# Expert weights in 2 MB transfers, in another order, with h2 stored as the gather reads it

## The reference

```python
logits = (x @ w_router + b_router)
top_vals, top_idx = lax.top_k(logits, TOP_K)            # 4 of 32 experts
wts = jax.nn.softmax(top_vals, axis=-1)
combine = jnp.sum(one_hot(top_idx, 32) * wts[..., None], axis=1)
def expert(acc, xs):
    wu, bu, wd, bd, g = xs                              # wu 1024 x 2048, wd 1024 x 1024
    gu = x @ wu + bu
    gate, up = gu[:, :D_FF], gu[:, D_FF:]
    gate = jnp.minimum(gate, 7.0)
    up = jnp.clip(up, -7.0, 7.0)
    glu = gate * jax.nn.sigmoid(1.702 * gate)
    y = ((up + 1.0) * glu) @ wd + bd
    return acc + g[:, None] * y, None
```

## Time and profile before

| | us |
|---|---|
| median of three runs | 1164.95 (1164.49 to 1165.76) |
| the profiled execution, its own time | 1163.09 |
| its span, first to last instruction | 1161.3 |
| TensorE busy in the span | 1112.6 |
| VectorE, ScalarE, GpSimd busy | 330.3, 168.0, 63.2 |
| mean rate of the DMA engines | 395 GB/s |

### The profile page before, as it was taken

How to read it: one execution, slowest core, us unless ns; L and a number is a source line. 1 busy time by engine, 2 the same in 40 slices (tenths; PEclk the granted TensorE clock), 3 DMA queues, 4 the chain that set the end, 5 groups by cost and what they waited for, 6 DMA issues and landing times.

```text
span 1161.3 us, 14218 instructions
## 1 busy us (share of the span) xinstructions
PE 1112.6 (96%) x5882; PEld 564.9 (49%) x5882; DVE 330.3 (28%) x622; ACT 168.0 (14%) x303; POOL 63.2 (5%) x107
## 2 busy tenths in 40 slices
PE   7999999989999999999999999999999999999996
PEld 6977799844444444444444444444444444444432
DVE  4675886422121212121212121212121212121113
ACT  4453145210000000000000000000000000000001
POOL 5040000100000000000000000000000000000000
PEclk9999999999999999999999999999999999999999
DMA  9989987878999999999999999999999999999992
GB/s 309 377 236 349 389 292 319 342 303 343 390 432 431 430 431 432 432 433 433 431 432 432 431 431 429 430 432 433 433 433 431 433 430 432 431 430 428 432 420 99
DMA packets 42609, 459.28 MB, mean 395 GB/s; under 512 B 3508, under 2 KB 15864, under 8 KB 26728
## 3 DMA queue, kind: packets, MB, share of 16 engines
q1 hardware_dynamic: 40936, 455.12, 94.0%
q0 software_dynamic: 1168, 2.81, 0.9%
q10 hardware_dynamic: 464, 0.79, 0.2%
HBM read 457.12 MB, written 1.57 MB: 395 GB/s over the span
## 4 chain that ended last, share of the span: by engine, by line
PE 47%; DMA 46%; DVE 2%; SPq 2%; issue 1%; ACT 1%; POOL 1%; POOLq 0%; DVEq 0%; ACTq 0%
DMA arena<-in_w_down_dram 41%; PE ps L1744 19%; PE ps L1705 12%; PE ps L1685 3%; DMA ring<-in_w_in_dram 3%; PE ps L1733 2%; DMA ring<-in_w_ada_dram 1%; DMA ring<-in_rpb_dram 1%; PE ps L1439 1%; SPq L401 1%; PE ps L1440 1%; PE ps L1607 1%; PE ps L1441 1%; SPq L397 1%; PE ps L1631 1%
## 5 line engine op out<-in xcount | busy, mean ns | idle before, releaser
L1705 PE MATMUL ps<-ring,arena 128*64 128x512 f32 x2048 | 452.4, 594 | 0.8 <-ACT arena L824 0.8
L1705 PEld LDWEIGHTS ps<-ring,arena 128*64 128x64 f32 x2048 | 143.5, 137 | 267.7 <-issue 261.2
L1744 PE MATMUL ps<-arena,x 128*64 128x512 f32 x992 | 219.2, 594 | 21.1 <-DMA arena<-in_w_down_dram 21.0
L1744 PEld LDWEIGHTS ps<-arena,x 128*64 128x64 f32 x992 | 70.6, 137 | 168.2 <-issue 133.4
L1685 PE MATMUL ps<-arena 128*128 128x128 f32 x512 | 124.9, 398 | 0.0
L1685 PEld LDWEIGHTS ps<-arena 128*128 128x128 f32 x512 | 121.9, 328 | 1.2 <-issue 1.2
L1243 DVE TENSOR_SCALAR arena<-iota,cur 128x128 f32<-128x128 f32 x64 | 19.3, 344 | 286.2 <-PE ps L1715 283.0
L1250 DVE TENSOR_SCALAR x<-ps 128x512 f32<-128x512 f32 x32 | 22.1, 692 | 257.0 <-PE ps L1705 257.0
L1265 DVE TENSOR_TENSOR late<-ps,gtf 128x512 f32<-128x512 f32 x64 | 41.2, 686 | 145.3 <-PE ps L1744 145.3
L615 POOL COPY selbuf<-sel 96x64 bf16 (+1 forms) x32 | 21.3, 665 | 871.4 <-DVE x L1251 868.9
L1733 PE MATMUL ps<-late,arena 64*128 64x512 f32 x264 | 65.9, 617 | 1.5 <-DVE late L1265 1.5
(11 more groups left out here) (267 smaller groups left out, 861.0 us busy)
## 6 DMA issues: line engine op xcount, KB each, us to landing
ring<-in_w_up_dram SPq DMA_DIRECT2D x58, 4096.0 KB, 27.1
arena<-in_w_down_dram SPq DMA_DIRECT2D x29, 4096.0 KB, 21.8
ring<-in_w_up_dram SPq DMA_DIRECT2D x12, 2048.0 KB, 12.4
ring<-in_w_ada_dram SPq DMA_DIRECT2D x16, 1024.0 KB, 10.8
ring<-in_w_ada_dram SPq DMA_DIRECT2D x16, 512.0 KB, 10.1
ring<-in_w_in_dram SPq DMA_DIRECT2D x16, 512.0 KB, 9.7
ring<-in_w_in_dram SPq DMA_DIRECT2D x8, 1024.0 KB, 7.5
arena<-in_w_down_dram SPq DMA_DIRECT2D x3, 2048.0 KB, 13.3
```

Source lines behind the costliest of these rows:

```text
L1705: ins = mm(ps[CAP * h:CAP * h + CAP, half, :].rearrange("q (p j) -> q p j", j=4), xgT[:, place, kk, CAP * a:CAP * a + CAP], w[:, half, :, ...
L1744: ins = mm(ps[CAP * n:CAP * n + CAP, YB, :], hT[:, j, CAP * h:CAP * h + CAP], w[:, jj, n * HALF:(n + 1) * HALF], start=(jj == 0), stop=(jj ...
```

## The change

Four edits go together.

1. All expert transfers up to D(30)'s first half are halves, 2 MB with runs of 16 KB. A half is issued when its own half of the place is free, and has its own semaphore: TensorE waits for the second half of U at kk = 2 and 6 and for the second half of D between the halves of `down`.
2. The order is U(e,0), U(e,1) for rising e, with D(e) after chunk u = 2e + `ahead(e)`, where u counts the chunks of w_up: after U(e+2,1) for e below 4, after U(e+2,0) for 4 to 9, and after U(e+1,1) from 10 on, which is the order in which TensorE reads them.
3. `h2` is stored with the columns dealt by j, so that the gather's weights are 128 adjacent floats; ScalarE's copy and `h2_out` write with a step instead.
4. After `up(0)` TensorE goes on to `up(1)`. `turn_hidden(0)`, the gather that stood after expert 0 (now into the bank of `down`'s result, YB) and, in the first round, the first scatter stand between the block rows of `up(1)`. The fixed parts of the loops change with it: 8 experts ahead of the loop and 4 behind it.

```diff
-HALVED = {(0, 0): 0, (0, 1): 0, (1, 0): 0, (1, 1): 0, (2, 0): 1, (E_LAST, 1): 1}
-FIRST_BODY = 4
+FIRST_BODY, LAST_BODY = 8, 4
+EVEN_FROM, EVEN_TO = 10, E - 4
+UP_HALVES = [(e, c) for e in range(E_LAST + 1) for c in range(2)]
+DOWN_HALVES = list(range(E_LAST))
+def ahead(e):
+    return 5 if e < 4 else 4 if e < EVEN_FROM else 3
+def order(first, last):
+    chunks = []
+    for u in range(2 * first, 2 * last):
+        chunks.append(("up", u // 2, u % 2))
+        chunks += [("down", e, None) for e in range(1, E) if 2 * e + ahead(e) == u]
+    return chunks
...
-                def up_whole(e, parity, c, after):
-                    sp.wait_ge(moe_free, after)
-                    sp.dma_start(up_chunk(parity, c).rearrange("p a b -> p (a b)"),
-                                 w_up_v[e, :, c, :]).then_inc(up_loaded[2 * parity + c][0], 16)
-                def down_whole(e, after):
-                    sp.wait_ge(moe_free, after)
-                    sp.dma_start(down_buf.rearrange("p a b -> p (a b)"), w_down_v[e, :, :]).then_inc(down_loaded[0], 16)
+                def up_whole(e, parity, c, at):
+                    for h in range(2):
+                        sp.wait_ge(moe_free, at + (2 * c + h + 1))
+                        sp.dma_start(up_chunk(parity, c)[:, 2 * h:2 * h + 2, :].rearrange("p a b -> p (a b)"),
+                                     w_up_v[e, :, c, 2 * h * SLOT:2 * (h + 1) * SLOT])\
+                            .then_inc(up_loaded[2 * parity + c][h], 16)
+                def down_whole(e, at):
+                    for h in range(2):
+                        sp.wait_ge(moe_free, at + (5 + h))
+                        down_part(e, 4 * h, 4 * h + 4, down_loaded[h])
+                def fixed(chunks):
+                    for kind, e, c in chunks:
...
+                fixed(order(2, EVEN_FROM + 2))
                 with sp.Fori(0, LOAD_LOOPS) as i:
...
                     for h in range(LOAD_BODY):
-                        steady(e0 + h, h, at0 + 6 * h)
+                        for c in range(2):
+                            up_whole(e0 + (h + 2), h, c, at0 + 6 * h)
+                        down_whole(e0 + (h + 1), at0 + 6 * (h + 1))
+                fixed(order(EVEN_TO + 2, E)[:-1])
...
-                        ins = nc.scalar.activation(h2[:, t, :].rearrange("p (a b) -> p a b", a=2),
-                                                   ps[:, 2 + 2 * t:4 + 2 * t, :], ACT.Copy)
+                        ins = nc.scalar.activation(h2[:, t, :].rearrange("p (a j q) -> p a q j", a=2, j=4),
+                                                   ps[:, 2 + 2 * t:4 + 2 * t, :].rearrange("p a (q j) -> p a q j", j=4),
+                                                   ACT.Copy)
...
-                V.scalar_tensor_tensor(out=h2[:, t, c], in0=ps[:, AF_BANK[k], :], scalar=rstd[:, t:t + 1],
-                                       in1=h2[:, t, c], op0=ALU.mult, op1=ALU.add).then_inc(h2_ready, 1)
+                by_row = h2[:, t, c].rearrange("p (j q) -> p q j", j=4)
+                V.scalar_tensor_tensor(out=by_row, in0=ps[:, AF_BANK[k], :].rearrange("p (q j) -> p q j", j=4),
+                                       scalar=rstd[:, t:t + 1], in1=by_row, op0=ALU.mult,
+                                       op1=ALU.add).then_inc(h2_ready, 1)
...
-                        ins = mm(ps[:, bank, j * P:(j + 1) * P], h2[:, t, HALF * c + j:HALF * (c + 1):4],
+                        ins = mm(ps[:, bank, j * P:(j + 1) * P], h2[:, t, HALF * c + j * P:HALF * c + (j + 1) * P],
...
-                    if kk % 4 == 2 and (e, c) in HALVED:
-                        per = 2 if c == e % 2 else 1
-                        pe.wait_ge(up_loaded[2 * (e % 2) + c][1], 16 * (r * per + HALVED[e, c] + 1))
+                    if kk % 4 == 2:
+                        pe.wait_ge(up_loaded[2 * (e % 2) + c][1], laps)
...
+                    elif e == 1:
+                        if kk == 2:
+                            turn_hidden(g - 1)
+                        if kk == 4:
+                            gather(r * PAIRS + 2, 0, YB)
+                        if kk == 5 and r == 0:
+                            scatter(g - 2, scat_done)
+                        if kk == 6:
+                            turn_weights(g - 1)
...
             def step(e, g, n, laps, loads, r):
                 up(e, g, laps, r, r == 0 and e == 0)
-                if e:
-                    down(e - 1, g - 1, loads)
+                if not e:
+                    return
+                if e == 1:
+                    pe.wait_ge(xg_ready, g + 2)
+                down(e - 1, g - 1, loads)
```

More of the change, by code:

```diff
@@ new lines, in down_whole @@
+                def down_whole(e, at):
[4 more added lines that the diff above has]
+                    for kind, e, c in chunks:
+                        if kind == "up" and (e, c) in UP_HALVES:
+                            for h in range(2):
+                                sp.wait_ge(moe_free, R + freed(e - 2) + 2 * c + h + 1)
+                                up_part(e, c, h)
+                        elif kind == "up":
+                            up_whole(e, e % 2, c, R + freed(e - 2))
+                        elif e in DOWN_HALVES:
+                            for h in range(2):
+                                sp.wait_ge(moe_free, R + freed(e) + 5 + h)
+                                down_part(e, 4 * h, 4 * h + 4, down_loaded[h])
+                        else:
+                            down_whole(e, R + freed(e))
@@ L447, in stream @@
                 first_free = [(O_done, 1), (kv_stored, 32), (unit_ready, 24), (unit_ready, 24), (br_done, KB),
                               (unit_ready, 28), (unit_ready, 32), (out_done, KB)]
-                order = [(0, 0, 0), (0, 0, 1), (0, 1, 0), (0, 1, 1), (1, 1, 1), (1, 0, 1), (1, 0, 0), (1, 1, 0)]
-                for (s, count), part in zip(first_free, order):
+                parts_of = [(0, 0, 0), (0, 0, 1), (0, 1, 0), (0, 1, 1), (1, 1, 1), (1, 0, 1), (1, 0, 0), (1, 1, 0)]
+                for (s, count), part in zip(first_free, parts_of):
@@ L457, in stream @@
                     down_part(0, 4 * h, 4 * h + 4, down_loaded[h])
[L458 to L470, removed]
+                fixed(order(2, EVEN_FROM + 2))
                 with sp.Fori(0, LOAD_LOOPS) as i:
-                    e0 = sp.snap(i * LOAD_BODY + 2)
-                    at0 = sp.snap(i * (6 * LOAD_BODY) + (R + freed(2)))
+                    e0 = sp.snap(i * LOAD_BODY + EVEN_FROM)
+                    at0 = sp.snap(i * (6 * LOAD_BODY) + (R + freed(EVEN_FROM)))
                     for h in range(LOAD_BODY):
-                        steady(e0 + h, h, at0 + 6 * h)
[L477 to L482, removed]
+                        for c in range(2):
+                            up_whole(e0 + (h + 2), h, c, at0 + 6 * h)
+                        down_whole(e0 + (h + 1), at0 + 6 * (h + 1))
+                fixed(order(EVEN_TO + 2, E)[:-1])
                 sp.wait_ge(moe_free, R + freed(E - 2) + 5)
@@ L848, in step @@
                 if e < E - 2:
-                    xg_out(g + 3, e % 2, (e // 2) % 2, 0)
+                    xg_out(g + 3, e % 2, (e // 2) % 2, 0 if e else YB)
             def experts(r):
@@ L864, in experts @@
                         step(FIRST_BODY + h, g0 + h)
-                for e in range(E - FIRST_BODY, E):
+                for e in range(E - LAST_BODY, E):
                     step(e, R + e)
@@ L1767, in up @@
                 if not first:
-                    pe.wait_ge(xg_ready, g + 2 if e < E - 1 else g + 1)
+                    pe.wait_ge(xg_ready, g + 1 if e in (1, E - 1) else g + 2)
                     bias(g)
@@ L1806, in step @@
                     gather(n, e % 2, 0)
-                if e or r == 0:
-                    scatter(g - 1, scat_done)
+                scatter(g - 1, scat_done)
             def fixed(r, e):
@@ L1814, in fixed @@
                 both = [(down_loaded[0], 16 * (r * T + e), 8)]
[L1815 to L1819, removed]
+                if e - 1 in DOWN_HALVES:
+                    nth, per = half_loads(e - 1)
+                    second = (down_loaded[1], 16 * (r * per + nth))
+                    both = [(down_loaded[0], 16 * (r * T + e), 4), second + (8,)]
+                    if e == T:
+                        both = [both[0], second + (6,), (tail_loaded[0], once, 8)]
                 if e == E:
@@ L1837, in experts @@
                         step(FIRST_BODY + h, g0 + h, n0 + h // 2, laps0 + 16 * (h // 2),
-                             [(down_loaded[0], loads0 + 16 * h, 8)], r)
-                for e in range(E - FIRST_BODY, E):
+                             [(s, loads0 + 16 * h, j1) for s, j1 in zip(down_loaded, (4, 8))], r)
+                for e in range(E - LAST_BODY, E):
                     step(e, *fixed(r, e), r)
```

6 lines of the change are left out of this document (4 added, 2 removed).

## The result

The changed kernel takes 1150.62 us (median, 1148.87 to 1151.47) beside 1164.85 us before: ratio 0.9875, 95% interval 0.9858 to 0.9892, faster by 14.2 us. The forecast was 1143 (1135 to 1158). The profiled execution takes 1148.87 us, its span is 1146.9.

The account below looks back on a forecast made before the run. The weight DMA queue bounds the kernel: 235.7 (D(0) landed) + 0.6 idle + 875.3 for 179 halves + 14.9 gives 1126.5 us; tail 2.1 and 11.0 make span 1139.6, profiled 1141.4, median 1143 (1135 to 1158).

Parts of the forecast that it names:

- The bound and its period: Expert phase: the DMA queue bounds; a 2 MB half takes 4.89 us (4.857 to 4.95), the period is 29.3 us.
- The slow rival: Expert weight stream: 16 KB runs cost more than the bound, 5.01 us a half loses all gain; 10 in 100.
- The start of a transfer: Queued weight transfers: rival that each pays a lone transfer's start, 7.4 us a half, 1600 us; 1 in 100.
- The gather: Gather matmuls on TensorE: contiguous weights save 1.65 us each (0 to 2.0), TensorE's period falls from 27.93 to 26.3.
- My rival: Early experts: gather no cheaper or up(1) stalls, queue idle 7 us instead of 0.6, 1150 us; 10 in 100.
- The writes of h2: Ahead of expert 0: strided writes hide; ScalarE's copy costs 0, h2_out at most 0.4 us more each.
- The walk of the early part: First experts, issue by issue: halves land 4.89 us apart, almost every issue in time, instead of 12.6 us lost.
- 0.6 idle: DMA queue in the first experts: total idle 0.6 us, from issues 0.4 and 0.2 us late.
- the rival of the clock: TensorE's waits at both halves of D lower the clock, period 29.7 us, about 1148 us; 5 in 100.
- 2.5 us of lead: DMA queue: a half issued 2.5 us before the one ahead lands leaves no gap; later, it lands 7.4 after issue.
- the first rival pair: The two milder rivals: gather no cheaper or up(1) stalls (1150 us, 10 in 100); clock (about 1148, 5 in 100).
- The tail: Kernel end: the last down is done 2.1 us after the last landing instead of 11.1, then 11.0 us as before.

Follow-up runs that it names:

- runs8_odd: Changed kernel with 2 MB w_up transfers of experts 4 to 30 holding alternate block rows, 8 KB runs that cannot join; 1159.65 us, ratio 0.9955.
- no_h2: Changed kernel without its third edit: h2 in order, gather reading with a step of 4; 1156.58 us, ratio 0.9944.
- before: The kernel before the change, beside which all others are timed; 1164.85 us in the main comparison.
- order_only: Changed kernel without its third and fourth edits, so only 2 MB halves and new order; 1156.18 us, ratio 0.994.
- before_h2: The kernel before with the third edit alone, h2 stored as the gather reads it; 1158.15 us, ratio 0.9959.
- early_gather: Changed kernel with the gather inside up(1) moved ahead of its bias, into the wait for selbuf; 1146.97 us, ratio 0.9855.
- after_again: The changed kernel itself run once more beside the kernel before; 1149.38 us, ratio 0.9874.
- old_order: Changed kernel with the transfer order of the kernel before from expert 10 on, D(e) after U(e+2,0); 1154.54 us, ratio 0.9916.
- best: Changed kernel with the gather of up(1) ahead of its bias and whole 4 MB w_up chunks for experts 4 to 30; 1143.8 us, ratio 0.9821.

## Why the prediction was right, point by point

**The bound and its period: right.** The queue sets the steady part; 4.89 us was taken for a half and 4.894 measured. The bounds by the nearest rows (32 KB and 8 KB runs) enclosed it, and `runs8_odd` shows what the upper row was a measure of. The slow rival (5.0 us or more) fell. The 6.2 us between D(29) and the half behind it, which spoke for it, is no price of changing between up and down: in the steady part of the changed kernel every half behind such a change lands 4.9 us after the one ahead. What it is stays open; the last section has what the traces show.

**The start of a transfer: no rival here.** Queued halves cost 4.894 us each. The fit of the Trainium skill (DMA: Bandwidth & Descriptors, "Anatomy of one DMA — SWDGE (gpsimd) path"), taken for each queued transfer, would give 6.8 us, an estimate from that page's figures. The trace disagrees with it for queued transfers issued by SP.

**The gather: right, mis-sized on the good side.** 1.95 us saved each instead of 1.65 (4.00 to 2.05), TensorE's period, read from the issues of D(2) and D(3) (298.5 and 324.5), 26.0 instead of 26.3. As forecast it counts only where the queue runs empty: `no_h2` loses 8 us by its ratio, all before D(2), and 5.4 without the late start of its trace. My rival put 7 us (1150 against 1143) on it.

**The writes of h2: the step failed.** "ACT's copy of h2 is earlier and hides under the output projection: 0." The copy doubled to 2.06 us, twice, and did not hide. From its start to the issue of D(0) it is 17.5 us in `before`, `order_only` and `no_h2`, where the copy is plain, and 18.7 in `before_h2` and the changed kernel, where it is not: 1.25 us, by the edit alone. D(0) is issued 1.1 us later and lands 0.7 later. `h2_out` went from 0.74 to about 1.06 us each and hid, as forecast: from the issue of D(0) to the first gather it is 6.8 us in both kernels. The Trainium skill, SBUF — State Buffer, section "Door 1: The DMA port swizzle", says that each access which goes to a new 16-byte line pays; the trace agrees for the copy (2.06 against 1.02 us) and, turned round, for the gather's weights (192 ns a load against 328).

**The walk of the early part: the mechanism right, the term "0.6 idle" mis-sized.** It measured 4.4. Two things lengthened it. First, the rival of the clock did come, in a place where I had not put it: behind the 2.44 us wait ahead of up(1), not behind the waits for D; it cost 1.7 us and put the issue of U(3,0) at 253.3 instead of 251.1. Second, and this is what failed, I took 2.5 us of lead (how long a half is issued before the one ahead of it lands) as enough for a queued half. By that rule the measured issues give no hole at all: 253.3 + 7.4 = 260.7 against 256.0 + 4.9, and 265.1 + 7.4 = 272.5 against 267.7 + 4.9. But U(3,0) and U(3,1), issued 2.7 and 2.6 us ahead, came 1.9 and 2.4 us late. The windows show a reason: the rate fell to 249 GB/s in 253.5 to 256.0 and to 203 in 265.0 to 267.5, so part of the 16 engines had run out of work up to 2.5 us before the half ahead had landed, and the lead that I counted was not theirs. `early_gather` issues both halves 4.7 and 4.8 us ahead and closes both holes.

A lead is no sharp bound, though, and one landing proves little. In `no_h2` halves issued 3.8 and 3.9 us ahead landed 4.7 and 6.5 us after the ones before them. In `after_again`, the same kernel as here, U(3,0) had 3.5 us of lead and no hole, U(3,1) 1.6 and one of 1.4 us, and four other halves came 0.4 to 1.6 us late. Only the total repeats: D(2) landed 82.5 us after D(0) there and 82.7 here. So the first rival pair (up(1) stalls; the clock) came true in part within the likeliest case.

**The tail: right.** 2.7 us after the last landing instead of 2.1, against 11.1 before; `old_order` loses 6.3 us of it again in its trace.

**The sum.** Span 1146.9 against 1139.6, 7.3 us: 0.7 from the later D(0), 3.8 from the holes, 2.0 between D(2) and the last landing (799.2 us to the first half of D(30) instead of 797.1; of this 1.4 in one place, at 486.8 us), 0.6 and 0.2 in the tail. The gain was 14.2 us of the 21.9 forecast.

## What to carry to other kernels

Where a queue of transfers is the bound, walk it issue by issue from the last moment when it was full: a stall of the engine that frees buffers is paid only if it brings an issue too near to the landing of the transfer before. Here 2.6 us was too near and 4.7 was enough; between them the traces do not agree. Price transfers by packets, from rows with longer and with shorter runs, and give the smaller transfers only to the places where a buffer must be handed back early. A layout that makes one side's reads contiguous makes the other side's writes strided: look up who is queued behind that writer.

## What the runs showed of the hardware

**Landings of 6.2 us, and packets of instructions.** The second half of D(8) of the changed kernel landed 6.3 us after the one ahead (454.9 + 25.6 = 480.5, 459.8 + 27.0 = 486.8), though the queue was full: the DMA share was 1.00 and the rate 421 GB/s. The DMA view of the window 480.5 to 486.8 of the changed kernel, then of 1108.25 to 1114.5 of the kernel before, the 6.2 us of its U(31,1), then of 511.3 to 516.2 of the changed kernel (queue, packets, MB, share of 16 engines):

```profile
q8 instruction: 1, 0.02, 1.1%
```

```profile
q8 instruction: 1, 0.02, 1.0%
```

```profile
q8 instruction: 1, 0.02, 1.4%
```

The first two hold one packet of the instruction queue, 16 KB, and so does the 6.2 us gap in `early_gather`. But the third holds one as well, and its half landed 4.9 us after the one ahead. Taken landing by landing from 280 to 1094 us, the changed kernel has 14 such packets: 13 beside landings 4.87 to 4.91 us apart, one beside the 6.29. So these gaps come with such a packet, and most such packets come without a gap. The packet alone is not the cause, and what else it takes stays open. It wasn't tried to move such a load.

**The clock.** A wait of TensorE of 1.3 us between matmuls left the granted clock at 1.00. Behind waits of 2.1 to 2.4 us it mostly fell for some microseconds to the lower level, 1.2 GHz (granted 0.51 in 248 to 250 of the changed kernel; 0.69 in 640 to 644 of `best`, so for a part of the stretch): in `best` 32 matmuls take 8.78 us behind a wait of 2.11 and 7.09 behind one of 1.32.

```profile
640.29 8.78 PE L1732 MATMUL ps<-ring,arena 128*64 128x512 f32 x32 [2.11 <-DMA ring<-in_w_up_dram]
...
669.51 7.09 PE L1732 MATMUL ps<-ring,arena 128*64 128x512 f32 x32 [1.32 <-DMA ring<-in_w_up_dram]
```

It is no rule without exception: behind another wait of 2.11 us in `best`, at 874.1 us, the 32 matmuls take 7.09 too. The queue hides the loss in `best`. In the changed kernel, at 248 us, nothing did.

**A lone half lands 7.3 to 7.4 us after its issue, and a half issued a little before the queue runs empty can take 9.5 to 9.9.** In `no_h2` one issued 2 us ahead took 7.3, so the lead alone does not decide it; the rest stays open.
